# One plain channel pair instead of three ahead of the seven-product pairs, in the up projection of a hybrid block

## What is computed

```python
h = rms_norm(x, norm_ffn_pre[l])
up = causal_dwconv(jnp.einsum('bsd,df->bsf', h, ffn_w_up[l]), ffn_conv_w[l]) + ffn_conv_b[l]
gate, val = jnp.split(up, 2, axis=-1)
ff = jnp.einsum('bsf,fd->bsd', jax.nn.silu(gate) * val, ffn_w_down[l])
x = x + rms_norm(ff, norm_ffn_post[l])
```

## Time and profile before

| | us |
|---|---|
| median of 3 runs | 1015.94 |
| lowest, highest | 1015.90, 1020.04 |
| the profiled execution | 1017.69 |
| its span, first to last instruction | 1015.9 |
| PE busy in the span | 998.1 (98%) |
| DVE busy | 612.9 (60%) |
| ACT busy | 407.9 (40%) |
| POOL busy | 158.3 (16%) |
| mean granted TensorE clock | 0.995 of full |

### The profile page before, as it was taken

One profiled execution on the slowest core, in us unless ns is written; L12 is line 12 of the kernel. 1 busy time (PEld: TensorE's weight loads), 2 busy tenths in 40 slices (PEclk: granted clock), 3 DMA queues, 4 the chain that ended last, 5 costly groups with the idle time before them and its releaser, 6 DMA issues.

```text
span 1015.9 us, 11938 instructions
## 1 busy us (share of the span) xinstructions
PE 998.1 (98%) x4580; PEld 809.2 (80%) x4580; DVE 612.9 (60%) x641; ACT 407.9 (40%) x624; POOL 158.3 (16%) x143
## 2 busy tenths in 40 slices
PE   8999999999999998999999999999999999999997
PEld 7988777777888886788888888888887888888886
DVE  5646786664554579777777677677654323344454
ACT  5525444443342344344444444444433222323342
POOL 2200000000111822332232242242200000000001
PEclk9999999999999999999999999999999999999999
DMA  6510110016223221232232222223216343455543
GB/s 218 152 57 28 42 42 22 25 59 207 84 102 100 69 83 59 66 104 84 63 98 83 68 89 79 81 75 91 104 63 218 127 152 130 149 197 186 184 168 124
DMA packets 84911, 104.90 MB, mean 103 GB/s; under 512 B 3849, under 2 KB 63489, under 8 KB 84865
## 3 DMA queue, kind: packets, MB, share of 16 engines
q1 hardware_dynamic: 84737, 104.20, 31.0%
q0 software_dynamic: 128, 0.07, 0.0%
HBM read 84.33 MB, written 19.92 MB: 103 GB/s over the span
## 4 chain that ended last, share of the span: by engine, by line
PE 92%; DVE 3%; DMA 2%; ACT 1%; POOL 1%; issue 1%; SPq 0%; DVEq 0%; POOLq 0%; ACTq 0%
PE ps L1441 29%; PE ps L1443 29%; PE ps L1442 29%; PE ps L1451 1%; PE ps L1549 1%; PE ps L1572 1%; DMA wraw<-in_w_in 1%; PE ps L1550 1%; PE ps L1558 1%; PE ps L1576 1%; DMA wraw<-in_w_o 1%; DMA act_in<-act_dram 0%; DVE w2lo L1316 0%; DVE hlo L992 0%; PE ps L1587 0%
## 5 line engine op out<-in xcount | busy, mean ns | idle before, releaser
L992 DVE TENSOR_TENSOR wlo<-wraw,whi 128x1024 fp32r<-128x1024 f32 x60 | 75.1, 1253 | 145.5 <-ACT whi L633 145.5
L633 ACT ACTIVATE whi<-wraw 128x1024 fp32r<-128x1024 f32 x60 | 63.4, 1058 | 180.1 <-PE ps L1443 176.2
L1441 PE MATMUL ps<-whi,ahi 128*128 128x512 f32 x320 | 127.7, 399 | 0.9 <-DVE alo L1269 0.9
L1443 PE MATMUL ps<-whi,alo 128*128 128x512 f32 x320 | 126.1, 394 | 0.0
L1442 PE MATMUL ps<-wlo,ahi 128*128 128x512 f32 x320 | 125.5, 392 | 0.0
L1441 PE MATMUL ps<-hhi,whi 128*128 128x512 f32 (+1 forms) x256 | 97.4, 381 | 2.0 <-DVE hlo L1010 2.0
L1443 PE MATMUL ps<-hhi,wlo 128*128 128x512 f32 (+1 forms) x256 | 94.7, 370 | 0.0
L1442 PE MATMUL ps<-hlo,whi 128*128 128x512 f32 (+1 forms) x256 | 94.7, 370 | 0.0
L563 POOL TENSOR_SCALAR meansq<-sumsq 128x1 f32<-128x1 f32 x28 | 7.6, 271 | 535.2 <-ACT x2b L804 244.9
L595 POOL TENSOR_TENSOR w_sums<-wraw 128x1024 f32<-128x1024 f32 x19 | 46.9, 2468 | 260.6 <-DVE h2lo L1316 106.3
L1443 PEld LDWEIGHTS ps<-whi,alo 128*128 128x128 f32 x320 | 60.1, 188 | 15.5
(11 more groups left out here) (196 smaller groups left out, 2215.9 us busy)
## 6 DMA issues: line engine op xcount, KB each, us to landing
wraw<-in_ffn_w_up SPq DMA_DIRECT2D x44, 512.0 KB, 4.9
wraw<-in_ffn_w_down SPq DMA_DIRECT2D x44, 512.0 KB, 3.4
act_dram<-yv SPq DMA_DIRECT2D x22, 512.0 KB, 2.6
act_in<-act_dram SPq DMA_DIRECT2D x42, 256.0 KB, 3.5
wraw<-in_w_in SPq DMA_DIRECT2D x14, 512.0 KB, 3.8
xin<-in_x SPq DMA_DIRECT2D x8, 512.0 KB, 4.5
wraw<-in_w_o SPq DMA_DIRECT2D x8, 512.0 KB, 3.3
xres<-in_x SPq DMA_DIRECT2D x8, 512.0 KB, 3.9
```

The source lines that it names most:

```text
L633: act.activation(hi[:, slot, :], wraw[:, base % RAW, :], ACT.Copy)\
L992: dve.tensor_tensor(lo[:, slot, :], wraw[:, base % RAW, :], hi[:, slot, :], ALU.subtract).then_inc(w_split, 1)
L1441: pe.matmul(acc, w_hi, x_hi, start=first, stop=False, skip_group_check=looped)
L1443: return pe.matmul(acc, w_lo, x_hi, start=False, stop=last, skip_group_check=looped)
```

## The change

PLAIN goes from 3 to 1, so that pairs 1 and 2 are done with seven products too (SEVEN = 21). Since the first pair with seven products is now pair 1, the differences of h2 are made and split right after h2 is complete, ahead of the convolution of pair 0: DVE takes quarter 3 over from POOL (POOL adds quarters 0, 2, 1), makes all differences in one go, splits them and the four entries of the first seven-product pair, and only then adds the taps of pair 0. Its silu and its gate times value stand inside the first turn of the loop. The ring of entries starts at place 4 (`RING_FROM`), in `whi`. On PE nothing changes but the counts and a wait dropped for pair 1, whose banks nobody has used in this stage.

```diff
-PLAIN = 3
+PLAIN = 1
+RING_FROM = 4
...
-            at = (4 * q + i) % RING
+            at = (4 * q + i + RING_FROM) % RING
...
-            for i, out in ((0, 0), (3, 2), (2, 1), (1, 3)):
+            for i, out in ((0, 0), (2, 1), (1, 3)):
                 whole_quarter(i, out)
...
+            def start_plain(val):
+
+                act.wait_ge(up_done, val + 1)
+                if val == 0:
+                    act.activation(yg[:, 0, :], banks(0), ACT.Identity, bias=ffn_bias(0),
+                                   scale=ffn_tap(2, 0)).then_inc(yg_started, 1)
+                else:
+                    act.activation(yv[:, 0, :], banks(2), ACT.Identity, bias=ffn_bias(NF),
+                                   scale=ffn_tap(2, NF)).then_inc(yv_started, 1)
...
-            plain_step(0)
-            plain_step(1)
             round_difference(0)
             round_entry(0, 0)
+            start_plain(0)
+            round_difference(1)
+            round_difference(2)
             round_entry(0, 1)
-            round_difference(1)
-            plain_step(2)
-            round_difference(2)
+            round_difference(3)
+            start_plain(1)
             round_entry(0, 2)
             round_entry(0, 3)
-            round_difference(3)
...
+                if q == 0:
+                    start_silu(0)
...
-            plain_step(0)
+            dve.wait_ge(ht_split, 2 * NT)
+            dve.wait_ge(wo_done, NT)
+            hi, lo = (block_of(h, 3).rearrange("p t k c -> p t (k c)") for h in (h2hi, h2lo))
+            finish_step(dve.tensor_tensor(made(2), hi, lo, ALU.add))
+            dve.wait_ge(quartered, 1)
+            dve.tensor_tensor(made(0), made(0), made(2), ALU.subtract).then_inc(r_made, 1)
             dve.wait_ge(quartered, 2)
-            dve.tensor_tensor(made(0), made(0), made(2), ALU.subtract).then_inc(r_made, 1)
-            plain_step(1)
+            finish_step(dve.tensor_tensor(made(2), made(1), made(2), ALU.subtract))
             dve.wait_ge(r_made, 1)
-            dve.wait_ge(quartered, 3)
-            finish_step(dve.tensor_tensor(made(2), made(1), made(2), ALU.subtract))
             dve.scalar_tensor_tensor(made(1), made(0), -1.0, made(1), ALU.mult, ALU.subtract)\
                .then_inc(r_made, 1)
             low_difference(0)
-            low_entry(0, 0)
-            low_entry(0, 1)
             dve.wait_ge(r_made, 2)
-            dve.wait_ge(quartered, 4)
+            dve.wait_ge(quartered, 3)
             dve.scalar_tensor_tensor(made(3), made(1), -1.0, made(3), ALU.mult, ALU.subtract)\
                .then_inc(r_made, 2)
+            low_entry(0, 0)
             low_difference(1)
-            plain_step(2)
+            low_entry(0, 1)
             low_difference(2)
             low_entry(0, 2)
             low_entry(0, 3)
             low_difference(3)
+            gate_taps(0)
+            value_taps(0)
...
+                if q == 0:
+                    gate_value(0, 1.0)
```

More of the change, by code:

```diff
@@ L852, in round_entry @@
                     act.wait_ge(seven_done, 7 * (before // 4) + ENTRY_LAST[before % 4])
-                elif (4 * q + i) % RING >= 2:
-                    act.wait_ge(up_done, 2 * PLAIN)
+                else:
+                    act.wait_ge(up_done, 2 * PLAIN - (4 * q + i == 0))
+                    if 4 * q + i >= RING - RING_FROM + 2:
+                        act.wait_ge(r_made, 2)
                 if i in (0, 3):
@@ L871, in keep @@
                 act.wait_ge(seven_done, 7 * q + which + 1)
-                if which == 0:
+                if which == 0 and pair >= 2:
                     act.wait_ge(act_ready, pair - 1)
-                if which == 2:
+                if which == 2 and pair >= 2:
                     act.wait_ge(act_saved[pair % 2], 16 * (pair // 2))
@@ L1285, in gate_value @@
                                          ALU.mult, ALU.mult).then_inc(act_ready, 1)
[L1287 to L1294, removed]
             def made(i):
@@ L1684, in _ @@
                 g0, g1, v0, v1 = pair_banks(pair)
-                pe.wait_ge(up_freed, 2 * pair - 2)
+                if pair >= 2:
+                    pe.wait_ge(up_freed, 2 * pair - 2)
                 seventh(q, 1, 0, 0, block_of(h2hi, 0), block_of(h2lo, 0), v0, True)
```

## The result

| | before | after |
|---|---|---|
| median, us | 1016.49 (4 runs) | 1030.43 (4 runs) |
| lowest, highest | 1015.90, 1020.04 | 1029.62, 1032.03 |
| ratio | 1 | 1.0127, 95% interval 1.0108 to 1.0146 |
| span of the profiled execution | 1015.9 | 1027.8 |
| end of h2 to the first matmul of the down projection, in the profile | 429.68 | 443.37 |

A forecast was written before the change was run, and what follows sets the result against it. TensorE was taken as the bound, holding 92% of the chain. Seam 25.7 us, less today's 5.5 and 6.4 for matmuls, gave 13.8 (13.9 by the other reckoning): 1015.9 + 13.9 = 1029.8 us, range 1024.5 to 1033.0.

The forecast's parts named there:

- The matmuls removed: PE, two pairs changed from plain (22.5 us) to seven products (19.3 us each, 0.2295 a matmul): 6.4 us saved.
- Turns between DVE and POOL: After h2: instructions reading two SBUF operands exclude each other and alternate; queue 31.1 us, PE starts pair 1 19.4 late.
- The seam as a whole: PE's lost time between plain and seven-product stages: 25.7 us after the change against 5.5 before.
- The rest of the seam, piece by piece: PE waits after pair 1's start: 0.6, 1.6 and 2.7 us ahead of products 2, 3, 7; 1.4 in pair 2.
- The clock: Rival, 12%: PE starts pair 1 at half clock; a third product at half pace adds 2.6 us, giving 1032.4.
- Edits at nothing: Weight splits, moved quarters, added sums, copies and folds, ring start and SP's save were put at no cost.
- The range: Whole-kernel time of 1024.5 to 1033.0 us, holding the forecast, the clock and DVE's turns.
- no turns: Rival, 5%: this order of DVE and POOL arrivals does not block; pair 1 starts at about 352.4, kernel 1013.0 us.
- DVE keeps its turn: Rival, 8%: DVE goes again when its next instruction follows at once; difference 3 comes 4.5 us earlier, kernel 1025.4.

The follow-up runs named there:

- experiment 1: Changed kernel with DVE's four h2 difference instructions cut to 8 of 512 columns, result not the reference's; ratio 1.0067 against the kernel before.
- Experiment 4: Changed kernel with 78 dummy matmuls on PE ahead of pair 1's first product, same result; ratio 1.0138 against the kernel before.
- experiment 6: The changed kernel run again, unchanged, on the same chip beside another kernel; 1030.77 us, ratio 1.0137 against the kernel before.
- experiment 3: Changed kernel with POOL's three quarters replaced by ACT copies of h2's rounded part, not full precision; ratio 1.0015 against the kernel before.
- experiment 2: Changed kernel with entry 0 of pair 1 rounded and split ahead of the differences, same result; ratio 1.0148 against the kernel before.

## Why the prediction was right, step by step

- *The matmuls removed*: the pace of 0.2295 came out, so the 6.4 us did.
- *Turns between DVE and POOL*: right, and shown apart from its rival by experiment 1. The list came in the order forecast. Pair 1 starts at H + 32.1 (363.56 less 331.43); the working had 365.6 less 333.2, 32.4.
- *The seam as a whole*: by starts, product 3 of pair 2 comes 50.4 us after PE has finished pair 0 (344.39 to 394.81); less 24.8 for nine products that is 25.6 us of seam, for 25.7 in the working.
- *The rest of the seam, piece by piece*: product 7 at H + 53.7 (forecast 53.9), product 3 of pair 2 at H + 63.4 (forecast 63.6). Between them the picture differed: the waits of 0.6 and 1.6 ahead of products 2 and 3 did not appear, because PE ran slower there, and the wait ahead of product 7 is 1.8 (and 0.16 of overlap) instead of 2.7. Experiment 4 brings them back, 0.4, 1.1 and 2.6.
- *The clock* was a rival of 12% for what it might cost; the half clock itself came, and its cost in the end was nil. The windows of the changed kernel (columns as in rows 10) show the half clock last until 369.2:

```profile
349.00:363.56 14.56, 0.01 (x1) 0.01 (x1) 14.53 (x6) 3.08 (x3) 11.06 (x4) 0.51 0.00 0
363.56:369.20 5.64, 5.64 (x13) 4.45 (x14) 5.55 (x4) 5.64 (x6) 0.00 (x0) 0.50 0.00 0
```

  The working had two whole products, 24 matmuls, at half pace for 5.5 us. It was 13 at 0.43 us, which put the first two products 2.9 us behind full pace. They end at 372.0, H + 40.6, where product 3 had been forecast at H + 40.1. That half microsecond is gone in the wait ahead of product 7. Experiments 4 and 6 show the same start of product 7 (H + 53.9 and H + 53.6) with no half clock and with a shorter one.
- *Edits at nothing*: after 394.81 PE has no wait until the down projection, and from its first matmul to the end it takes 253.0 us in both kernels.
- *The range* was 8.5 us wide for a time that fell 0.6 us from the forecast. The rival "no turns" is refuted by every DVE record between 338 and 362, and "DVE keeps its turn" by each from 344.87 on, where a POOL instruction is served between two of DVE's that follow at once. The rows of before were enough for that, and 5% and 8% were generous. That the medians' difference meets the forecast to 0.1 us is in part luck, since their interval is 4 us wide; the 13.7 from H is the better test, and there the starts of products 1, 3 and 7, and of product 3 of pair 2, are each right to 0.5 us, while product 2 and the waits between are not.

What the forecast did not say: that the wait is divided as 13 us for POOL's quarters and 6 for the rest (experiment 3), and that starting product 1 early is worth nothing (experiment 2).

## What to carry to other kernels

Where two lists are put side by side that use DVE with two SBUF inputs and POOL at once, add up the instructions of both, not the longer of the two: in these traces each waits for the whole of the other's current instruction, so a short instruction behind a long POOL one is the worst case (4.52 us for 32 elements a row). Before cover is cut to save matmuls, lay the preparation that it hides end to end, and compare: here 31 us against 13. And take the stretch between two marks of the trace, not the whole span, when the rest of the program varies by more than the effect.

## What the runs showed of the hardware that was not expected

The half clock outlasted the idle stretch by 5.6 us (363.56 to 369.20) in one profile of the changed kernel and by 3.3 us in the other (experiment 6); in the trace of before, at another place, the half clock lasted 3.4 us.

In four of the experiments the clock also fell to half at product 7 of pair 1, after waits there of 1.9 us (experiment 1, from 381.5), 2.0 (experiment 2, from 389.5), 2.1 (experiment 3, from 375.3) and 2.6 (experiment 4, from 389.4, after three shorter waits of 1.5, 0.4 and 1.1 us). The changed kernel's wait of 1.8 us at the same place, the 2.6 us in its second profile, and before's of 3.3, 0.7 and 0.9 us brought no fall. The row of experiment 4's windows:

```profile
388.00:392.00 4.00, 3.65 (x11) 2.94 (x12) 4.00 (x4) 0.56 (x1) 3.84 (x3) 0.68 0.00 0
```

So the length of the wait alone does not decide it, and what does was not tried. In these four runs all but 0.2 us of what the fall cost is taken up by product 3 of pair 2: none has the wait of 1.3 us ahead of product 3 of pair 2 that both profiles of the changed kernel have.
